# Input and first output projection in split form, attention 1 among the gelu branch's chunks, norms as factors at eviction, last chunks by token half

## What is computed

```python
# block 1
u = rms_norm(x, g_mix_pre) @ w_in                       # 2048 -> 5120
q, k, v, xr, yg = split(u, [1024, 2048, 3072, 4096])    # each 1024 wide
attn = neighborhood_attention(q, k, v, rpb)             # 8 heads of 128, bias, softmax
rec = rglru_bidirectional(xr, ...) * gelu(yg)           # two gated linear scans over the tokens
mixed = concat([rms_norm(attn, g_attn_out), rms_norm(rec, g_rec_out)]) @ w_out
h = x + rms_norm(mixed, g_mix_post)
fn = rms_norm(h, g_ffn_pre)
h = h + rms_norm((silu(fn @ w_gate) * (fn @ w_up)) @ w_down, g_ffn_post)   # 5632 wide
gate = sigmoid(rms_norm(h, g_ple_pre) @ w_ple_gate)
h = h + rms_norm(gate * (p @ w_ple_proj), g_ple_post)
# block 2
mod = silu(c) @ w_ada + b_ada                           # 2048 -> 6 x 2048
h = layer_norm(x) * (1 + sc1) + sh1
x = layer_norm(a*x + g1 * token_mix(h), ln1_g, ln1_b)   # dilated attention and latent attention
h = layer_norm(x) * (1 + sc2) + sh2
x = layer_norm(a*x + g2 * peer(h), ln2_g, ln2_b)        # top-16 of 16384 experts per head
```

## Time and profile before

| | us |
| --- | --- |
| median of three runs | 3594.81 (3594.74 to 3598.14) |
| profiled execution | 3603.56 |
| its span in the trace | 3602.0 |
| input projection, from first to last matmul | 28.2 to 330.4 |
| attention 1 | 330.4 to 361.9 |
| norms of the two branches | 361.9 to 385.5 |
| wout | 385.5 to 509.4 |
| norm, residual, norm, turn | 509.4 to 540.7 |
| gate/up | 540.7 to 1036.0 |

### The profile page before, as it was taken

The page is one execution under the profiler, slowest core; times in us unless marked ns, Lnnn a source line. Parts: engine busy times, 40 slices in busy tenths (PEclk is TensorE's granted clock), DMA queues, the critical chain, the costliest instruction groups (busy, mean ns, idle before and its releaser), DMA issues.

```text
span 3602.0 us, 42919 instructions
## 1 busy us (share of the span) xinstructions
PE 3317.0 (92%) x15906; PEld 2611.5 (73%) x15906; DVE 1967.7 (55%) x2283; ACT 1221.4 (34%) x1263; POOL 823.4 (23%) x535
## 2 busy tenths in 40 slices
PE   7998779999999979789877799999999899999996
PEld 6874338888888844434556799888888688888885
DVE  4233457788865535550256579555555455555555
ACT  1122024444434420100242333455555343443431
POOL 2000000000000000000001478887888600100010
PEclk9999889999999989889988899999999899999998
DMA  7433547777755566579224256666666666666663
GB/s 257 141 123 111 187 152 272 273 278 279 277 191 191 198 234 247 219 273 358 75 84 163 94 179 178 211 216 214 210 212 216 181 248 235 244 240 242 238 246 116
DMA packets 194539, 747.53 MB, mean 208 GB/s; under 512 B 53873, under 2 KB 53905, under 8 KB 124321
## 3 DMA queue, kind: packets, MB, share of 16 engines
q1 hardware_dynamic: 129696, 664.84, 51.8%
q0 software_dynamic: 55552, 64.91, 6.7%
q10 hardware_dynamic: 9216, 16.78, 1.3%
HBM read 710.62 MB, written 35.83 MB: 207 GB/s over the span
## 4 chain that ended last, share of the span: by engine, by line
PE 69%; POOL 16%; DVE 8%; issue 4%; DMA 2%; ACT 2%; POOLq 0%; ACTq 0%; DVEq 0%; SPq 0%
POOL weight_dram L2107 15%; PE bank L435 15%; PE bank L581 10%; PE bank L582 10%; PE bank L583 10%; PE bank L587 9%; PE bank L419 7%; PE bank L588 5%; DMA weight_dram<-misc 1%; PE bank L372 1%; PE bank L850 1%; PE bank L484 1%; DVE aux L1916 0%; POOL part_lo L2087 0%; DMA misc<-in_w_ada 0%
## 5 line engine op out<-in xcount | busy, mean ns | idle before, releaser
L1880 DVE TENSOR_TENSOR part_lo<-ring,part_hi 128x2048 fp32r<-128x2048 f32 x248 | 568.0, 2293 | 406.5 <-ACT part_hi L1343 386.9
L1343 ACT ACTIVATE part_hi<-ring 128x2048 fp32r<-128x2048 f32 x252 | 482.8, 1916 | 550.9 <-PE bank L583 293.9
L2107 POOL DMA_INDIRECT weight_dram<-misc x256 | 571.1, 2231 | 101.6 <-issue 95.2
L587 PE MATMUL bank<-h_both,part_hi 128*128 128x512 f32 x1664 | 579.6, 392 | 8.1 <-DVE part_lo L1880 8.1
L435 PE MATMUL bank<-ring,xT 128*128 128x512 f32 (+1 forms) x1216 | 510.7, 581 | 8.0 <-DVE xT L1543 6.3
L587 PE MATMUL bank<-h_both,ffn_hi 128*128 128x512 f32 x1408 | 493.7, 397 | 4.8 <-DVE ffn_lo L1643 4.8
L588 PE MATMUL bank<-h_both,part_lo 128*128 128x256 f32 x1664 | 467.1, 281 | 0.0
L435 PEld LDWEIGHTS bank<-ring,xT 128*128 128x128 f32 x1216 | 226.9, 192 | 291.7 <-issue 289.9
L581 PE MATMUL bank<-part_hi,coef_hi 128*128 128x512 f32 x1024 | 399.7, 390 | 17.6 <-DVE part_lo L1880 17.6
L582 PE MATMUL bank<-part_lo,coef_hi 128*128 128x512 f32 x1024 | 399.4, 390 | 0.0
L583 PE MATMUL bank<-part_hi,coef_lo 128*128 128x512 f32 x1024 | 399.3, 390 | 0.0
(11 more groups left out here) (315 smaller groups left out, 4415.4 us busy)
## 6 DMA issues: line engine op xcount, KB each, us to landing
ring<-in_u_table SPq DMA_DIRECT2D x128, 1024.0 KB, 4.9
ring<-in_v_table SPq DMA_DIRECT2D x128, 1024.0 KB, 4.8
ring<-in_stream SPq DMA_DIRECT2D x114, 1024.0 KB, 6.3
misc<-in_w_ada SPq DMA_DIRECT2D x192, 512.0 KB, 5.7
ring<-in_gateup SPq DMA_DIRECT2D x88, 1024.0 KB, 4.9
ring<-in_down SPq DMA_DIRECT2D x44, 1024.0 KB, 4.8
ring<-in_wo_pq SPq DMA_DIRECT2D x32, 1024.0 KB, 4.8
weight_dram<-conv_tmp POOLq DMA_DIRECT2D x1, 16384.0 KB
```

Source lines behind the costliest of these rows:

```text
L587: nc.tensor.matmul(out[:, 0:2 * S], hi, x_pair, start=start, stop=False)
L1343: a.activation(part_hi[j % PARTS], raw[j % RAW], ACT.Copy).then_inc(sem("hi_ready"), 1)
L1880: v.tensor_tensor(part_lo[j % PARTS], raw[j % RAW], part_hi[j % PARTS].bitcast(F32), ALU.subtract).then_inc(sem("lo_ready"), 1)
L2107: g_.indirect_dma_start(out=places, out_offset=bass.IndirectOffsetOnAxis(ap=gstage[:, t, k:k + 1], axis=0), in_=wstage[:, t, k:k + 1], in_ ...
```

## The change

It does the following.

- **Input projection.** The order is xr, q, k, v, yg, and all 40 chunks are in split form through four raw and four `hi` slots; `lo` overwrites the raw slot (`lower_in`, `raw_lo`). SP waits for `multiplied` of chunk n - 4 before it loads chunk n. x goes to `nat`; DVE norms half 0 and ACT half 1; the turned x is split into `x1_hi` and `x1_lo`. The gate products stand among the chunks (direction 0 after chunks 2 to 9, direction 1 after 16 and 20). The recurrence takes an exponential on ACT in place of the reciprocals of 2048 columns. x is loaded again into `resid` by POOL after chunk 39.
- **Embedding projection.** It moves to the start, among the turns of x, is stored in memory and read back by POOL when down's activations are ready.
- **Attention 1.** Its heads are spread over the yg chunks, one for each: values of head h - 1 in the middle of chunk h, scores of h + 2 and turn of h behind it (`PacedPE`, with `PacedDVE` and `PacedACT`). Probabilities are scaled before the turn.
- **Norms as factors.** wout is split by its input, heads part first (8 chunks), then the recurrence part (8), in 16 outputs. The attention's and the recurrence's root-mean-square are applied when wout's outputs are evicted (`mixed1`, `mixed_in`), not before the product. The last three chunks run by token half, and the norms behind them too (`half_roots`). The h3 turns stand among the first gate/up chunk's matmuls.
- **Modulation.** `ADA_EARLY` is 2: two groups in wout, ten in gate/up, four in pgate, eight from lat on, two of them after qk2.
- **Gate/up.** The raw load waits for `multiplied` of chunk j; `lo` overwrites the raw slot; DVE takes the two modulation rows first and then makes the lower part of chunk c + 3.
- **Down, end.** Down's raw loads wait for `multiplied`. The last four value chunks run by token half, and DVE's norm of a half waits for that half's bank (`mixed_out`). The result goes to `xT`.

```diff
-ADA_EARLY = 4
+ADA_EARLY = 2
...
-PHASES = [("xr", 8), ("yg", 8), ("q", 8), ("k", 8), ("v", 8), ("wout", 16), ("gateup", 2 * KF), ("down", DOWN),
-          ("pproj", 2), ("pgate", 16), ("lat", 8), ("kr", 1), ("qk2", 16), ("v2", 8), ("mla", 7), ("wo", 16),
...
+PHASES = [("xr", 8), ("q", 8), ("k", 8), ("v", 8), ("yg", 8), ("wout", 16), ("gateup", 2 * KF), ("down", DOWN),
+          ("pgate", 16), ("lat", 8), ("kr", 1), ("qk2", 16), ("v2", 8), ("mla", 7), ("wo", 16), ("pq", 16)]
...
+            for n in range(24):
+                stationary_chunk(pe, ("xr", "q", "k")[n // 8], n % 8, x1_hi, x1_lo)
+                if 2 <= n < 10:
+                    gates(0, n - 2)
...
+            for h in range(NH):
+                stationary_chunk(pe, "yg", h, x1_hi, x1_lo, between=(lambda: at1.values(h - 1)) if h else None)
+                if h + 2 < NH:
+                    at1.scores(h + 2)
+                at1.turn(h)
...
+            for n in range(N_IN + 1, N_IN + 13):
+                if n == N_IN + 8:
+                    pe.wait_ge(sem("rec_lo_out"), RB)
+                wout_chunk(n).then_inc(multiplied, 1)
+                if n in (N_IN + 1, N_IN + 6):
+                    mean((n - N_IN) // 6)
+                if n == N_IN + 9:
+                    ada_sum(0)
+            for n in range(N_IN + 13, N_IN + 16):
+                m = wout_chunk(n, (0,))
+                if n % 2:
+                    m.then_inc(sem("mixed_half"), 1)
...
-                        sp_.wait_ge(sem("lo_ready"), j + 1 + 8 * it)
+                        sp_.wait_ge(multiplied, SPLIT_GU + j + 1 + 8 * it)
...
-            for c in range(4):
-                product_n(pe, "pproj", c // 2, 2 * c, 1, 2, lambda k, t: pT[:, k, t * P:(t + 1) * P], sub=c % 2,
-                          last=(c % 2 == 1))
...
+            for g in range(ADA_W2 + 6, ADA_G):
+                ada_sum(g)
...
-            for j in range(NEB - PARTS, NEB):
-                values_of_block(j, 0, stop=j == NEB - 1)
+            for t in range(T):
+                for j in range(NEB - PARTS, NEB):
...
```

More of the change, by code:

```diff
@@ new lines, in moving_chunk @@
+        def moving_chunk(n, out, lhs_hi, lhs_lo, first, last, halves=range(T), between=None):
+            for k in range(4):
+                if k == 2 and between:
+                    between()
+                ks = slice(k * BAND, (k + 1) * BAND)
+                for t in halves:
+                    m = split_products(out(t)[:, :], lhs_hi(k, t), lhs_lo(k, t), ffn_hi[n % PARTS][:, ks],
+                                       raw_lo[n % RAW][:, ks], first and k == 0, last and k == 3)
+            return m
@@ new lines, in _, with gates @@
+            pe.wait_ge(sem("ple_copied"), 8)
+            pe.wait_ge(sem("n1_lo_out"), KD)
+            def gates(z, b):
+                if z == 0 and b == 0:
+                    pe.wait_ge(sem("rg_in"), 16)
+                pe.wait_ge(sem("conv_done"), b + 1)
+                n = z * RB + b
+                if n >= 4:
+                    pe.wait_ge(sem("gates_taken"), n - 3)
+                for g in range(2):
+                    m = pe.matmul(bank[4 + n % 4][:, g * S:(g + 1) * S], rg_w[:, z, g, b, :], xcT[:, b, :],
+                                  start=True, stop=True)
+                m.then_inc(sem("gates"), 1)
@@ L847, in ada_sum, with mean @@
+            def mean(part):
+                pe.wait_ge(sem("heads_summed"), part + 1)
+                for t in range(T):
+                    m = pe.matmul(bank[5][:, 2 * part + t:2 * part + t + 1], conv_tmp[:, part, t * P:(t + 1) * P],
+                                  ones[:, 0:1], start=True, stop=True)
+                m.then_inc(sem("means"), 1)
             def ada_sum(g):
@@ L1606, in ada_row, with some_ada @@
                     sem("mod_ready"), 1)
-            with steps.loop(ADA_EARLY, 0) as it:
-                for k in range(KD):
-                    ada(k, it)
-                ada_end(it)
-                ada_row(it)
-            v.wait_ge(taken, out_no("gateup", 0))
-            sum_ssq()
-            roots(D, EPS)
-            v.wait_ge(sem("row_in"), 16)
-            add_normed(aux[:, 0, :], 0)
-            normed(8, "h3", "g_ffn_pre")
-            wait()
+            def some_ada(first):
+                for k in range(first, first + 4):
+                    ada(k % KD, k // KD)
```

973 lines of the change are left out of this document (670 added, 303 removed).

## The result

| | before | after |
| --- | --- | --- |
| median of six runs, us | 3595.91 (3594.68 to 3600.46) | 3608.04 (3605.94 to 3613.78) |
| span of the profiled execution, us | 3602.0 | 3604.4 |
| mean granted clock | 0.963 | 0.954 |

The ratio is 1.0034, 95% interval 1.0021 to 1.0047: a little slower, where 86.7 us less had been forecast, and outside the range of 3478 to 3540.

A forecast was written before the change was run, and what follows sets the result against it. TensorE (PE), busy 92% of the span, was taken as the bound. Terms -88.8 + 5 - 15.0 + 19.7 - 7.6 = -86.7 gave 3516.9 for the profiled execution; less 8.75, a median of 3508 us, range 3478 to 3540.

The forecast's parts named there:

- Price of a chunk: Split-form matmuls: stationary chunk 48 instructions 0.12 us apart, 5.8 us against 6.92; moving chunk 24 at 0.227, 5.45 us.
- Start: Beginning of the kernel: input chunk 0 starts at 38 instead of 28.15, +9.9 us, bounds 33 to 45.
- Input stage: Input projection to the end of v: chunk 0 at 38, gelu branch at 236.3, splitting work hidden behind the chunks.
- rival (F): Stationary input chunks: instructions 0.11 us apart, so the 32 chunks take 5.2 each; 3490 us, chance 1%.
- Rival (C): Input stage paced by DVE, through late slot refills or GpSimd's masks: chunks step at 7.1, +42, 3550 us; chance 7%.
- Attention: Attention 1 among the gelu branch's chunks: steps of 9.0 set by DVE and ACT, PE 8.2; eight steps 70.7 us.
- Rival (E): Paced heads delay every gelu chunk, so attention is only moved (step 17 instead of 9); within 0.2%, 3595 us; chance 1%.
- The term of -88.8: Everything up to the end of the first gate/up chunk: its eviction at 460.0 us instead of 548.8.
- Rival (A): Output stage nearer to PE's time: stops of 11, 4 and 7 us vanish; 3486 us, chance 20%.
- Gate/up: Raw load waits for chunk j's matmuls: load, rows and lower part take 16.15 of 16.89 us; +5, bounds 0 and +25.
- rival (B): Gate/up paced by modulation loads that land near 7.3 us instead of 5.6; 3531 us, chance 18%.
- rival (D): Slower than before through gate/up's load chain, deciding from landings of about 9.7 us; at 10.0, 3610 us; chance 3%.

The follow-up runs named there:

- the run with the wait alone: Kernel before, with one SyncE edit: gate/up's raw load waits until chunk j is multiplied instead of for its lower part; 3652.06 us, ratio 1.0151.

## Why the prediction was wrong, point by point

- **Price of a chunk.** 0.12 and 0.227 us held: in gate/up, in q and in wout the steps are those. A stationary chunk takes 5.95 rather than 5.8 (gate products left out: 90.78 to 96.73).
- **Start.** Chunk 0 at 43.1, expected 38, within the bounds 33 to 45. What I missed was the queue: the projection's second half behind raw chunk 0, beside GpSimd's own loads.
- **Input stage.** The gelu branch started at 250.1 instead of 236.3: 5.1 of it the start, 6.0 the stop behind GpSimd's masks; the other 2.7 lie in PE's busy time (201.0 for 198.3), about what 0.15 on each of 24 chunks makes. That is 0.124 an instruction, so rival (F) with its 0.11 was not borne out. Rival (C) named the masks as mechanism; its price of 42 was too high since it comes once.
- **Attention.** Eight steps took 67.1 (expected 70.7); the common step is 7.9, below even my figure for PE (8.2). DVE and ACT, whose pieces I had added up to a chain of 9.0, don't set it; which of these pieces lie beside one another I haven't worked out. Rival (E) falls too: attention 1 is hidden, not moved.
- **Output projection and norms.** 21.4 to the first mean (20.3 expected), 114.8 from there to the h3 turns (112.7), 12.2 to the end of the first chunk (15.5). The term of -88.8 came out as -82.6. Rival (A) was not borne out: behind the first mean the stops are 2.8, 2.7, 2.1, 4.0 and 3.2 us, 14.8 together, where I had put 11 and 7; they lie elsewhere than I had them, since the one before the first modulation sum is 4.0 and not 11. (The 4 that (A) names beside these stands in no term of my sum.) Which part of the change earned how much of it wasn't tried by runs.
- **Gate/up: the step that failed.** The term was +5, with bounds 0 and +25; it came out as +88.2, a step of 6.72 for each chunk, and so the sign that I had named for being wrong (more than 0.2 off 5.7) came true. I priced the moved wait through one consumer, the lower part, three chunks ahead, and gave that chain 16.15 of 16.89 us. That chain holds: PE's waits for lower parts are 4.5 us in the run with the wait alone and 3.0 in the changed kernel with only the sum moved. But the modulation load behind the raw load on SP has a second consumer, PE's own sum, which stands ahead of chunk 1 of the next round, one chunk behind the group's last load. For it the chain is 0.6 to the issue, 5.6 landing and 0.2 to the start, 1.5 for the rows and 2.5 for the lower part and the activation that now stand ahead of DVE's sign-off: 10.4, against 5.4 of PE's work. I had followed the late load to DVE's queue only, and had not gone on to what DVE's sign-off of a group releases. PE's own order, where the sum stands ahead of chunk 1 of each round, was the place to look. Landings were 5.5/5.7/7.2 over the stage, before 5.5/5.6/8.0 (the 6.7 in the prediction is the largest of a part of it). So rival (B), landings near 7.3, was not borne out, and rival (D), slower by landings of 9.7 and more, had the right stage and the wrong mechanism; that its 3610 is near the measured 3608 is luck.
- **The clock.** I charged the slow clock behind two long stops (2.5 and 2 us) and not in gate/up. There each stop of 5.1 costs 3.2 more (32.0 over ten), of which 0.9 is the sum itself at half speed (1.86 instead of about 0.95).
- **After down, latent turn, tail.** -15.1 (expected -15.0), +19.2 (+19.7), -7.3 (-7.6): right in size. In the tail the cause was half wrong, as shown.

With the load moved ahead, that is with the failed step mended, the profiled execution takes 3518.4 (span 3516.7) and the median is 3519.8; the prediction had 3516.9 and 3508. The first is near in part by luck: up to the end of the first gate/up chunk this run is 4.6 behind the forecast (84.2 gained for 88.8), and gate/up then costs 3.1 less (1.9 for 5). The second misses mostly by the 8.75 that I carried over from the kernel before, whose profiled execution lay above its median by that much, where this one lies 1.5 below.

## What to carry to other kernels

When a wait is moved, list every instruction queued behind it on its engine, and follow each to its last consumer, the engine's own rare ones (once per round) included: here the one with the fewest chunks between load and use decided, not the one that is used most. Place a sum or a small product where its input is already there, not at the tidy end of a loop; moving ten such sums by one chunk was worth 82 us, and six others 32. A short stop of PE costs more than its length by the clock behind it: here 2.3 us on top of 2.6, and 3.2 on top of 5.1.

## What the runs showed of the hardware

- **The clock.** In gate/up the mean granted clock was 0.94 with ten stops of 5.1 us and 1.00 without any; the same 2808 instructions took 528.2 and 496.0 us. With ten stops of 2.6 us it was 0.97 and 519.6. Behind a stop it fell to its lower level (1.2 GHz) and was back at the full one (2.4 GHz) some 3 us later, behind a stop of 5.2 us in the changed kernel as behind one of 2.7 in the run with the wait alone (0.50 between 852 and 854, 1.00 from 855 on). At full clock pairs of instructions start 0.35 us apart; behind the stop that ends at 845.6 the first two pairs take 0.81 and 0.54. Two stretches there:

```profile
845.60:848.00 2.40, 2.37 (x3) 0.59 (x4) 1.03 (x2) 2.11 (x2) 0.00 (x0) 0.50 0.26 101
849.00:850.00 1.00, 1.00 (x7) 0.90 (x6) 1.00 (x1) 0.98 (x2) 0.00 (x0) 1.00 0.00 0
```

- **One port for two engines.** A DVE operation on 16 columns takes 0.17 us alone and 2.3 to 2.4 beside a mask of GpSimd. The mask takes 2.45 when nothing holds it, 4.3 beside a lower part, and took 6.60 beside DVE's scan of 4.42.
- **Transfers at the start.** The first loads of SP's queue landed in the order of issue; three more behind one left its landing about the same (28.3 with them, 29.2 without), and one fewer ahead of it shortened the time from issue to landing by 5.4 us (25.1 to 19.7).
